# Stick-breaking attention regrouped into tiles of 4 query blocks by 512 keys, with the weights split into high and low parts for F32R products

## The chip, the cores and the metric

One core of one Trainium2 chip runs one launch of the kernel. The metric is the device time of that launch in microseconds (us). Everything is float32 in and out. F32R below is a reduced form of float32 that TensorE multiplies faster; where full precision is needed, the kernel keeps a number as a pair of F32R values, a high part and a low part (the remainder).

## The reference, cut to what matters

One layer of a hybrid encoder: 2048 tokens, width 1024. A projection feeds stick-breaking attention (8 heads of 64) and an mLSTM (4 heads of 128); both are gated, projected, normed and added, and a layer embedding is added last. The part that the change rewrites is the attention:

```python
for blk in range(s // SB_BLOCK):                      # 16 blocks of 128 queries
    q0 = blk * SB_BLOCK; k_end = q0 + SB_BLOCK
    z = jnp.einsum('bhqd,bhkd->bhqk', q[:, :, q0:k_end], k[:, :, :k_end]) * scale
    strict = s_pos < t_pos                            # a key strictly before its query
    log_beta = jax.nn.log_sigmoid(z)
    log_keep = jnp.where(strict, log_beta - z, 0.0)
    after = lax.cumsum(log_keep, axis=3, reverse=True) - log_keep
    a = jnp.where(strict, jnp.exp(log_beta + after), 0.0)
    outs.append(jnp.einsum('bhqk,bhkd->bhqd', a, v[:, :, :k_end]))
```

The cumulative sum runs over all keys of a query from the last to the first. A row that is cut into pieces of keys is therefore a chain: a piece begins with what the piece to its right ended with.

## The kernel before

The kernel is a row of stages, each a block in which five engines (TensorE = PE, VectorE = DVE, ScalarE = ACT, GpSimd = POOL, SyncE = SP for DMAs) run their own programs and meet at semaphores. `input_projection` multiplies the normed input by nine groups of 512 weight columns, as three F32R products each, and stores the results to DRAM. Groups 0 and 1 are queries and keys: ACT writes the high part (`evacuate_hi`), DVE the low part (`evacuate_lo`), and SP stores both (`store_qk`) from two staging buffers each. Group 2 is the values: `evacuate_copy` lets ACT and DVE copy alternate tiles, and SP stores them as rows of 2 KB into `proj_n`. A short block `prepare_mlstm` follows, then `stick_breaking_attention`, then `mlstm_and_output_projection`, then `layer_embedding`.

The attention works in units. A unit is one head, one block of 128 queries and up to 512 keys; a query block with more keys is cut into nearly equal pieces, taken from the right. There are 80 units for a pair of heads and 320 in all. A loop over the four pairs holds the code of 80 units (`pipeline`, with a part ahead of and behind the loop). At step n each engine works on units at fixed lags behind n:

- PE `score(n)`: two F32R products of queries with keys, 128 x 512, into one of four PSUM tiles `y`.
- ACT at lag 1: exp, then ln(1 + x), into `buf`.
- POOL at lag 2, for the first (rightmost) unit of a row alone: it adds `lowest` to the 128x128 diagonal block (line 708).
- DVE at lag 2: `softplus` (line 813), then `start`, which is one column: the negated last key (line 833) for a first unit, or what the unit to the right left, less the own last key (line 835).
- DVE at lag 3: `scan` (line 822), the running sum over the keys of the unit.
- POOL at lag 4, for first units: `lowest` is added once more (line 701).
- PE at lag 5: `turn` transposes every 128x128 block (line 734). ACT at lag 6: exp of the turned block into `aT` (line 786). PE at lag 7: `times_v` (line 761), for each block of keys a plain float32 product of `aT` (stationary) with the values of two heads, 128 columns. DVE at lag 8: a 128x64 copy of the finished output (line 849).

Each engine's queue is strictly in this written order. On DVE the order within a step is scan(n-3), softplus(n-2), start(n-2), and, where a row has ended, the copy. `score(u)` waits for `start(u-3)`, so for the scan of u-4, to free its tile `y`.

Of the kernel before, what the change touches and what calls it, by code (L numbers as in the profile page):

```python
# [43 lines left out]
def input_projection(nc, x, pre_norm_w, w_in, conv_w, conv_b, sb_norm_w, ml_norm_w, qk_hi, qk_lo, ml_t, proj_n,  # L44
# [8 lines left out]
    with ExitStack() as ctx:  # L53
# [140 lines left out]
        def _(sp):  # L194
# [12 lines left out]

            def store_first(q, j):
                store_qk(q - 1, j, slice(j * P, (j + 1) * P), bass.ds((q - 1) * GROUP, GROUP))
# [26 lines left out]
            with sp.Fori(0, TG) as m:  # L236
                for t in range(TG):
                    store_qk(m + TG, t, bass.ds((m + TG) * P, P), slice(t * GROUP, (t + 1) * GROUP))

# [9 lines left out]
            store(evacuated, 2, proj_n, 0, BANKS, 0)  # L249
# [3 lines left out]
            store(evacuated, 6, proj_n, 0, BANKS, 2 * GROUP)  # L253
            store(evacuated, 7, proj_n, 0, BANKS, 3 * GROUP)
            store(staged, 3, proj_n, 0, BANKS, 4 * GROUP)
# [4 lines left out]
            for t in range(BANKS):  # L260
                sp.wait_ge(stored[t], 16 * ((GROUPS - 2) * TG + 2))
            for i in range(2):
                sp.wait_ge(stored_hi[i], 16 * (4 * TG + 1))
                sp.wait_ge(stored_lo[i], 16 * (4 * TG + 1))

        @block.scalar
        def _(act):
# [38 lines left out]
            def evacuate_copy(g):  # L306
                def tile(m, t):
                    if t % 2 == 1:
                        act.wait_ge(out_ready, 4 * m + (16 * g + t + 2))
                        act.wait_ge(stored[t], 16 * m + (16 * ((g - 2) * TG + 1)))  # L310
                        nc.scalar.copy(stage[t], po[t][:]).then_inc(evacuated[t], 1)
                return tile

            def evacuate_gate(g, func):
                def tile(m, t):
                    act.wait_ge(out_ready, 4 * m + (16 * g + t + 2))
                    act.wait_ge(stored[t], 16 * m + (16 * ((g - 2) * TG + 1)))
                    nc.scalar.activation(stage[t], po[t][:], func).then_inc(evacuated[t], 1)
                return tile

            def evacuate_conv(g):
                def silu(m, t):
                    act.wait_ge(tap_done, TG * CONV_K * m + CONV_K * (TG * TG * (g - 4) + t + 3))
                    act.wait_ge(stored[t], 16 * m + (16 * ((g - 2) * TG + 1)))
# [32 lines left out]
            for g, evacuate in ((1, evacuate_hi(1, 1.0)),  # L357
                                (2, evacuate_copy(2)), (3, evacuate_gate(3, ACT.Silu)),
# [7 lines left out]
            for t in (1, 3):  # L366
                act.wait_ge(out_ready, 16 * GROUPS + (t + 2))
                act.wait_ge(stored[t], 16 * ((GROUPS - 2) * TG + 1))
# [3 lines left out]
        def _(dve):  # L372
# [37 lines left out]
            def evacuate_copy(g):  # L410
                def tile(m, t):
                    if t % 2 == 0:
                        dve.wait_ge(out_ready, 4 * m + (16 * g + t + 2))
                        dve.wait_ge(stored[t], 16 * m + (16 * ((g - 2) * TG + 1)))
# [56 lines left out]
            for g, evacuate in ((1, evacuate_lo(1, 1.0)),  # L471
                                (2, evacuate_copy(2)), (3, weigh_gate(3, gate_w[0])),
# [9 lines left out]
                if g == 4:  # L482
                    dve.wait_ge(conv_w_loaded, 16 * (CONV_K + 1))
                    for i in range(2):
                        dve.wait_ge(stored_hi[i], 16 * (4 * TG + 1))
                        dve.wait_ge(stored_lo[i], 16 * (4 * TG + 1))
                whole_group(dve.Fori, evacuate, (lambda ks: split(g + 1, ks)) if g < GROUPS - 1 else nothing)
            for t in (0, 2):
                dve.wait_ge(out_ready, 16 * GROUPS + (t + 2))
                dve.wait_ge(stored[t], 16 * ((GROUPS - 2) * TG + 1))  # L490
# [81 lines left out]
def stick_breaking_attention(nc, qk_hi, qk_lo, proj_n, y_sb, before, other_loads):  # L572

# [4 lines left out]
    with ExitStack() as ctx:  # L586
# [10 lines left out]
        BUFS, YS = 8, 4  # L597

        units = []
        for head in range(2):  # L600
            for i in range(TOK):

                parts = i // 4 + 1
                bounds = [(i + 1) * c // parts * P for c in range(parts + 1)]
                for c in reversed(range(parts)):
                    units.append((head, i, bounds[c], bounds[c + 1] - bounds[c], c == parts - 1, c == 0))
        UNITS = len(units)
        assert UNITS % BUFS == 0 and UNITS % YS == 0
        BEYOND_START = 4
        assert units[BEYOND_START][1] == 4  # L610
        firsts = [u for u in range(UNITS) if units[u][4]]

        E_LAG, SP_LAG, S_LAG, M_LAG, T_LAG, X_LAG, V_LAG, O_LAG = 1, 2, 3, 4, 5, 6, 7, 8

        def rank(u):

            return len(firsts) * (u // UNITS) + sum(f <= u % UNITS for f in firsts)

        def pipeline(fori, step):

            for n in range(O_LAG):
                step(0, n)
            with fori(0, PAIRS - 1) as it:
                for n in range(O_LAG, UNITS + O_LAG):
                    step(it, n)
            for n in range(O_LAG, UNITS + O_LAG):
                step(PAIRS - 1, n)

        def has(it, u):

            return u >= 0 and not (isinstance(it, int) and it == PAIRS - 1 and u >= UNITS)

# [3 lines left out]
        v = sb("b_v", [P, TOK, SB_WIDTH])  # L636
        buf = [sb(f"b_buf{s}", [P, GROUP]) for s in range(BUFS)]
        aT = [sb(f"b_aT{s}", [P, GROUP]) for s in range(2)]
        ident = sb("b_ident", [P, P])
        lowest = sb("b_lowest", [P, P])  # L640
# [3 lines left out]
        qk_loaded = [sem(f"qk_loaded{s}") for s in range(2)]  # L644
        start_loaded = sem("b_start_loaded")
        v_start_loaded = sem("b_v_start_loaded")
        v_loaded = sem("b_v_loaded")
# [3 lines left out]
        ln_masked = sem("ln_masked")  # L651
        sp_done = sem("sp_done")
        scan_done = sem("scan_done")
        log_done = sem("log_done")
        log_masked = sem("log_masked")
        turned_done = sem("turned_done")
        aT_done = sem("aT_done")
        av_done = sem("av_done")
        o_read = sem("o_read")
        def load_head(sp, s, head, cols, loaded):  # L660
            q, k = bass.ds(head * SB_DIM, SB_DIM), bass.ds(head * SB_DIM + SB_WIDTH, SB_DIM)
# [6 lines left out]
        def load_v(sp, tiles, loaded):  # L668
            rows = proj_n[tiles.start * P:tiles.stop * P, 0:SB_WIDTH]
            sp.dma_start(v[:, tiles, :], rows.rearrange("(j p) n -> p j n", p=P)).then_inc(loaded, 16)  # L670

        def prefetch(sp):

            load_head(sp, 0, 0, slice(0, GROUP), start_loaded)
            load_v(sp, slice(0, 4), v_start_loaded)
# [4 lines left out]
        o = [psum(f"b_o{s}", [P, P]) for s in range(2)]  # L680
# [3 lines left out]
        def _(pool):  # L684
            nc.gpsimd.memset(ident[:], 0.0).then_inc(zeroed, 1)
            nc.gpsimd.memset(lowest[:], 0.0).then_inc(zeroed, 1)
            pool.wait_ge(zeroed, 2)
# [3 lines left out]
            nc.gpsimd.affine_select(out=lowest[:], in_=lowest[:], compare_op=ALU.is_gt, fill=-BIG, base=0,  # L691
                                    pattern=[[-1, P]], channel_multiplier=1).then_inc(consts_ready, 1)
            pool.wait_ge(consts_ready, 2)

            def step(it, n):
                u = n - M_LAG
                if has(it, u) and units[u % UNITS][4]:
                    keys = units[u % UNITS][3]
                    own = buf[u % BUFS][:, keys - P:keys]
                    pool.wait_ge(log_done, it * UNITS + (u + 1 + YS))  # L700
                    nc.gpsimd.tensor_tensor(own, own, lowest[:], ALU.add).then_inc(log_masked, 1)  # L701
                n -= E_LAG
                if has(it, n) and units[n % UNITS][4]:

                    keys = units[n % UNITS][3]
                    own = buf[n % BUFS][:, keys - P:keys]
                    pool.wait_ge(ln_done, it * UNITS + (n + 1))
                    nc.gpsimd.tensor_tensor(own, own, lowest[:], ALU.add).then_inc(ln_masked, 1)  # L708

            pipeline(pool.Fori, step)  # L710

        @block.sync
        def _(sp):
            load_head(sp, 0, 0, slice(GROUP, SEQ), qk_loaded[0])
            load_v(sp, slice(4, TOK), v_loaded)
            load_head(sp, 1, 1, slice(0, SEQ), qk_loaded[1])
            other_loads(sp)
            with sp.Fori(1, PAIRS) as it:
                for s in range(2):

                    sp.wait_ge(y_done, (it - 1) * UNITS + UNITS // 2 * (s + 1))
                    load_head(sp, s, 2 * it + s, slice(0, SEQ), qk_loaded[s])

        @block.tensor
        def _(pe):
            def turn(it, u):
                keys, first = units[u % UNITS][3:5]
                if first:
                    pe.wait_ge(log_masked, it * len(firsts) + rank(u))
                else:  # L730
                    pe.wait_ge(log_done, it * UNITS + (u + 1 + YS))
                pe.wait_ge(aT_done, it * UNITS + (u + 1))
                for j in range(keys // P):
                    mm = pe.transpose(turned[u % 2][:, j * P:(j + 1) * P], buf[u % BUFS][:, j * P:(j + 1) * P],  # L734
                                      ident[:])
                mm.then_inc(turned_done, 1)

            def score(it, u):
                head, i, key0, keys, first, last = units[u % UNITS]
                very_first = isinstance(it, int) and it == 0  # L740
                if very_first and u == 0:
                    pe.wait_ge(start_loaded, 96)
                if u % UNITS in (0, UNITS // 2) and not (very_first and u == 0) or very_first and u == BEYOND_START:
                    pe.wait_ge(qk_loaded[head], 96 * it + (96 * (u // UNITS) + 96))
                pe.wait_ge(log_done, it * UNITS + (u + 1))
# [5 lines left out]
            def times_v(it, u):  # L751
                head, i, key0, keys, first, last = units[u % UNITS]
                if isinstance(it, int) and it == 0 and u == 0:
                    pe.wait_ge(v_start_loaded, 16)
                if u == BEYOND_START:
# [1061 lines left out]
```

## Time and profile before

| | |
|---|---|
| median of 3 runs | 2082.02 us (2081.91 to 2086.26) |
| span of the profiled execution | 2080.1 us |
| input projection | 0 to 856 us |
| preparation of the mLSTM | 856 to 872 us |
| attention | 872 to 1502 us |
| mLSTM and output projection | 1502 to 1826 us |
| layer embedding | 1826 to 2080 us |
| PE, DVE, ACT, POOL busy over the span | 93%, 53%, 42%, 12% |

The span runs from the first to the last instruction. The busy share of an engine is a mean over stages with different limits, so it is read stage by stage. PE's busy time counts a matmul from its start to its modelled end, and matmuls overlap; the spacing of the weight loads (PEld) tells more of its pace.

### The profile page before, as it was taken

What the parts mean: (1) busy time and instruction counts of PE and PEld (TensorE: products, weight loads), DVE (VectorE), ACT (ScalarE), POOL (GpSimd) and SP (SyncE); (2) the same over time, 40 slices, a digit from 0 to 9 for tenths busy, and PEclk for the clock granted to TensorE, in tenths of its full rate; (3) what the DMA queues carried; (4) which work ended last, traced back from release to release, by engine and by line L of the source; (5) the groups of instructions that cost most, each with busy time, mean ns of one, the idle gap of its engine ahead of it and who ended that gap; (6) DMA issues with size and microseconds to landing.
All of it is one profiled execution on the core that took longest, in us unless ns stands there. A gap on an engine that the chain in (4) does not pass through costs nothing. (4 is left out here: it accounts for less than half of the span.)

```text
span 2080.1 us, 31157 instructions
## 1 busy us (share of the span) xinstructions
PE 1937.3 (93%) x10348; PEld 1612.5 (78%) x10348; DVE 1105.3 (53%) x2017; ACT 869.2 (42%) x1729; POOL 258.2 (12%) x442
## 2 busy tenths in 40 slices
PE   6999999999999999599989989999889999979998
PEld 5888888887878888277877777777768888858887
DVE  4521111355511011289989989999866555443333
ACT  4311111222201121188878878888644444331111
POOL 2100000000000000112112112112013344300000
PEclk9999999999999999799999999999969999989999
DMA  4653221212122111352202202100064444332221
GB/s 163 181 163 100 98 77 59 86 46 86 51 90 87 50 46 50 92 140 62 49 15 62 46 19 62 43 20 1 25 194 127 152 151 151 132 134 91 72 87 41
DMA packets 89296, 176.91 MB, mean 85 GB/s; under 512 B 12388, under 2 KB 39204, under 8 KB 86484
## 3 DMA queue, kind: packets, MB, share of 16 engines
q1 hardware_dynamic: 84344, 156.48, 24.7%
q0 software_dynamic: 4832, 18.91, 2.6%
q8 instruction: 66, 1.08, 0.2%
q14 instruction: 54, 0.44, 0.1%
HBM read 112.35 MB, written 63.01 MB: 84 GB/s over the span
## 5 line engine op out<-in xcount | busy, mean ns | idle before, releaser
L822 DVE TENSOR_TENSOR_SCAN b_buf<-b_y,b_buf 128x511 f32<-128x511 f32 (+2 forms) x320 | 357.4, 1117 | 16.8 <-issue 9.1
L761 PE MATMUL b_o<-b_v,b_aT 128*128 (+1 forms) x2176 | 299.2, 277 | 5.3 <-DVE y_sb L849 5.2
L761 PEld LDWEIGHTS b_o<-b_v,b_aT 128*128 128x128 f32 x2176 | 270.3, 193 | 10.2 <-issue 5.2
L548 PE MATMUL a_po<-w_lo,uT_hi 128*128 128x512 f32 x640 | 249.8, 390 | 2.4 <-DVE w_lo L398 2.4
L548 PE MATMUL a_po<-w_hi,uT_lo 128*128 128x512 f32 x640 | 249.7, 390 | 0.0
L548 PE MATMUL a_po<-w_hi,uT_hi 128*128 128x512 f32 x640 | 249.6, 390 | 0.0
L748 PE MATMUL b_y<-kst,qst_lo 128*128 128x512 f32 (+2 forms) x320 | 149.4, 467 | 52.0 <-DVE b_buf L835 27.4
L786 ACT ACTIVATE b_aT<-b_turned 128x512 f32<-128x512 f32 (+2 forms) x320 | 169.7, 530 | 63.0 <-PE b_o L761 47.4
L790 ACT ACTIVATE b_buf<-b_y 128x512 f32<-128x512 f32 (+2 forms) x320 | 169.9, 531 | 59.6 <-PE b_y L749 55.2
L813 DVE SCALAR_TENSOR_TENSOR b_buf<-b_buf,b_y 128x512 f32<-128x512 f32 (+2 forms) x320 | 186.2, 582 | 11.2 <-POOL b_buf L708 11.2
L734 PE MATMUL b_turned<-b_ident,b_buf 128*128 128x128 f32 x1088 | 176.9, 278 | 11.5 <-issue 8.9
L793 ACT ACTIVATE b_buf<-b_buf 128x512 f32<-128x512 f32 (+2 forms) x320 | 181.2, 566 | 10.1
L734 PEld LDWEIGHTS b_turned<-b_ident,b_buf 128*128 128x128 f32 x1088 | 131.9, 142 | 51.7 <-POOL b_buf L701 21.2
L548 PE MATMUL a_po<-uT_hi,w_lo 128*128 128x512 f32 x384 | 150.3, 391 | 2.4 <-DVE w_lo L398 2.4
L548 PE MATMUL a_po<-uT_lo,w_hi 128*128 128x512 f32 x384 | 149.9, 390 | 0.0
L548 PE MATMUL a_po<-uT_hi,w_hi 128*128 128x512 f32 x384 | 149.9, 390 | 0.0
L548 PEld LDWEIGHTS a_po<-w_lo,uT_hi 128*128 128x128 f32 x640 | 120.4, 188 | 27.8 <-DVE w_lo L398 2.8
L548 PEld LDWEIGHTS a_po<-w_hi,uT_hi 128*128 128x128 f32 x640 | 120.5, 188 | 25.3
L548 PEld LDWEIGHTS a_po<-w_hi,uT_lo 128*128 128x128 f32 x640 | 120.6, 188 | 24.9
L1684 PE MATMUL d_product<-d_w_hi,d_hT_lo 128*128 128x512 f32 x320 | 127.0, 397 | 3.8 <-DVE d_w_lo L874 3.6
L748 PEld LDWEIGHTS b_y<-kst,qst_lo 128*128 128x128 f32 x320 | 61.5, 192 | 88.1 <-DVE b_buf L835 53.1
L1684 PE MATMUL d_product<-d_w_hi,d_hT_hi 128*128 128x512 f32 x320 | 125.3, 391 | 0.0
(195 smaller groups left out, 3088.4 us busy)
## 6 DMA issues: line engine op xcount, KB each, us to landing
proj_n<-x_in SPq DMA_DIRECT2D x80, 256.0 KB
w_raw<-in_w_in POOLq DMA_DIRECT2D x8, 2048.0 KB, 9.5
x_in<-in_x SPq DMA_DIRECT2D x16, 512.0 KB, 4.3
qk_hi<-stage_hi SPq DMA_DIRECT2D x32, 256.0 KB, 2.5
qk_lo<-stage_lo SPq DMA_DIRECT2D x32, 256.0 KB, 3.1
ml_t<-x_in SPq DMA_DIRECT2D x32, 256.0 KB
ring<-ml_t SPq DMA_DIRECT2D x16, 512.0 KB, 4.7
ring<-proj_n SPq DMA_DIRECT2D x16, 512.0 KB, 4.1
```

What stands on the lines that cost most here:

```text
L548: mm = pe.matmul(po[t][:], lhsT, rhs, start=(k == 0 and n == 0), stop=(k == KT - 1 and n == 2))
L734: mm = pe.transpose(turned[u % 2][:, j * P:(j + 1) * P], buf[u % BUFS][:, j * P:(j + 1) * P], ident[:])
L748: pe.matmul(out, qst_lo[head][:, q], k, start=True, stop=False)
L761: mm = pe.matmul(o[i % 2][:], aT[u % 2][:, j * P:(j + 1) * P], v[:, key0 // P + j, bass.ds((it + u // UNITS) * P, P)], start=(first and j ...
L786: nc.scalar.activation(aT[x % 2][:, 0:keys], turned[x % 2][:, 0:keys], ACT.Exp).then_inc(aT_done, 1)
L790: nc.scalar.activation(b, y[e % YS][:, 0:units[e % UNITS][3]], ACT.Exp).then_inc(e_done, 1)
L793: nc.scalar.activation(b, b, ACT.Ln, bias=1.0).then_inc(ln_done, 1)
L813: nc.vector.scalar_tensor_tensor(out=b, in0=b, scalar=LN_MAX, in1=y[u % YS][:, 0:keys], op0=ALU.min, op1=ALU.max).then_inc(sp_done, 1)
L822: nc.vector.tensor_tensor_scan(down, y[u % YS][:, 1:keys][:, ::-1], down, b[:, keys - 1:keys], ALU.add, ALU.subtract)\
L1684: mm = pe.matmul(product[b][:], a[s][:, k, :], w[:, k, half], start=(k == ks[0] and i == 0), stop=(k == ks[-1] and i == 2))
```

## The change

In `stick_breaking_attention` the order of the units changes: for each head and each group g of 4 query blocks, the chunks c of 512 keys are taken from the right, and within a chunk the 4 query blocks r. A first unit (c = g) has (r + 1) x 128 keys, all others have 512. It is still 40 units a head and 320 in all, with the same keys in all. 24 of 40 are chained to the unit 4 places back. Besides units there are jobs, 40 a head too: a job is one block of 128 keys by the 4 query blocks of its chunk, so up to 512 columns wide (512, 384, 256 and 128 in the diagonal chunk).

- `pipeline` is written out over all 320 units with no loop, and lags grow: 15 steps instead of 8.
- The causal mask: POOL's two additions per first unit go. PE adds `future` (BIG above the diagonal) to the tile `y` with one BF16 product per first unit, after ACT's exp has read it (`hide_future`); POOL sets one column with a memset (`mask_end`).
- DVE's one-column instruction: none for a first unit; for a chained one a `tensor_tensor` of two SBUF columns (`seed`). What the earlier unit left is put into `carry` by ACT (`carry_over`, one column, 192 times).
- After the exp of a job, POOL splits the 128 x up to 512 weights: a copy rounded to F32R (`hi`), then a subtraction (`lo`). PE multiplies with the pair of values as the stationary operand, two F32R products of up to 512 columns per job. The result `o` is 128 (high and low halves of 64) x 512 queries.
- When a group of query blocks ends, ACT copies `o` (`copy_o`), PE turns it with 4 transposes (`turn_o`), DVE adds the halves (`add_o`). It happens 32 times and takes the place of 128 copies.
- In `input_projection`, group 2 is evacuated as a pair like groups 0 and 1 and stored to `v_pair` in pieces of 256 bytes; the attention loads 1 MB of it per head, in pieces of 512 bytes, instead of 4 MB once.

The core of the diff (waits on `stored`, columns of `proj_n` and declarations of semaphores are left out):

```diff
+            def store_v(m, t):
+                i, n = t % 2, m + 2 * TG
+                rows = bass.ds((m * BANKS + t) * P, P)
+                sp.wait_ge(staged_hi[i], 2 * n + (t // 2 + 1))
+                sp.dma_start(v_pair[:, rows, 0, :].rearrange("h p d -> p h d"),
+                             stage_hi[i][:, 0:GROUP].bitcast(F32).rearrange("p (h d) -> p h d", h=SB_HEADS))\
+                    .then_inc(stored_hi[i], 16)
...
-                                (2, evacuate_copy(2)), (3, evacuate_gate(3, ACT.Silu)),
+                                (2, evacuate_hi(2, 1.0)), (3, evacuate_gate(3, ACT.Silu)),
...
-        BUFS, YS = 8, 4
+        BUFS, YS, PARTS = 12, 4, 3
...
+            for g in range(TG):
+                for c in reversed(range(g + 1)):
+                    for r in range(4):
+                        keys = (r + 1) * P if c == g else GROUP
+                        units.append((head, 4 * g + r, c * GROUP, keys, c == g, c == 0))
+                        r0 = r if c == g else 0
+                        jobs.append((head, 4 * c + r, r0 * P, c == g and r == 0, c == 0 and r == 3))
...
-        E_LAG, SP_LAG, S_LAG, M_LAG, T_LAG, X_LAG, V_LAG, O_LAG = 1, 2, 3, 4, 5, 6, 7, 8
+        E_LAG, F_LAG, SP_LAG, S_LAG, C_LAG, T_LAG, X_LAG, H_LAG, V_LAG, R_LAG, W_LAG, O_LAG = 1, 2, 2, 3, 4, 8, 9, 10, 12, 13, 14, 15
...
+            for n in range(PAIRS * UNITS + O_LAG):
+                step(n)
...
-                    nc.gpsimd.tensor_tensor(own, own, lowest[:], ALU.add).then_inc(log_masked, 1)
+            def split(m):
+                cols = slice(jobs[m % UNITS][2], GROUP)
+                raw, hi, lo = aT[m % 2][:, cols], a_hi[m % PARTS], a_lo[m % PARTS]
+                pool.wait_ge(aT_done, m + 1)
+                until(pool, av_done, (m - PARTS + 1))
+                nc.gpsimd.tensor_copy(hi[:, cols], raw).then_inc(hi_done, 1)
+                pool.wait_ge(hi_done, m + 1)
+                nc.gpsimd.tensor_tensor(lo[:, cols], raw, hi[:, cols].bitcast(F32), ALU.subtract).then_inc(lo_done, 1)
...
+            def hide_future(u):
+                    pe.wait_ge(e_done, u + 1)
+                    pe.matmul(y[u % YS][:, keys - P:keys], ident_b[:], future[:], start=False, stop=True,
+                              skip_group_check=True).then_inc(future_hidden, 1)
...
+                pe.matmul(o[:, col:], pair, a_lo[m % PARTS][:, col:], start=first, stop=False)
+                pe.matmul(o[:, col:], pair, a_hi[m % PARTS][:, col:], start=False, stop=last).then_inc(av_done, 1)
...
+            def step(n):
+                if has(n - C_LAG):
+                    carry_over(n - C_LAG)
+                if has(n - R_LAG):
+                    copy_o(n - R_LAG)
+                if has(n - X_LAG):
+                    weights(n - X_LAG)
+                if has(n - E_LAG):
+                    log_one_plus_exp(n - E_LAG)
...
-                    nc.vector.tensor_scalar_mul(last_key, last_key, -1.0).then_inc(log_done, 1)
...
+                if not units[u % UNITS][4]:
+                    last_key, before = buf[u % BUFS][:, GROUP - 1:GROUP], (u - 4) % 8
+                    dve.wait_ge(sp_done, u + 1)
+                    dve.wait_ge(carried, passed(carrying, u - 3))
+                    nc.vector.tensor_tensor(last_key, carry[:, before:before + 1], last_key, ALU.subtract)\
+                        .then_inc(seed_done, 1)
```

## Rows read from the trace of the kernel before

**Rows 1.** Stages: each engine's busy us (instructions), then TensorE clock, DMA share, GB/s.

```profile
872.00:1502.00 630.00, 562.61 (x3903) 481.60 (x3904) 587.41 (x1087) 496.42 (x961) 115.27 (x258) 0.97 0.21 48
```

**Rows 2.** Groups by shape in the attention: busy us, mean ns of one, idle before.

```profile
L822 DVE TENSOR_TENSOR_SCAN b_buf<-b_y,b_buf 128x511 f32<-128x511 f32 x160 | 204.4, 1278 | 4.8 <-DVE b_buf L833 0.9
L835 DVE SCALAR_TENSOR_TENSOR b_buf<-b_y,b_buf 128x1 f32<-128x1 f32 x192 | 42.0, 219 | 6.8
L786 ACT ACTIVATE b_aT<-b_turned 128x512 f32<-128x512 f32 x160 | 95.5, 597 | 40.7 <-PE b_o L761 36.2
```

**Rows 3.** DVE in order of time in the middle of the attention: start, us, instruction.

```profile
1246.11 0.22 DVE L835 SCALAR_TENSOR_TENSOR b_buf<-b_y,b_buf 128x1 f32<-128x1 f32 x1
1246.36 1.01 DVE L822 TENSOR_TENSOR_SCAN b_buf<-b_y,b_buf 128x383 f32<-128x383 f32 x1
1247.29 0.66 DVE L813 SCALAR_TENSOR_TENSOR b_buf<-b_buf,b_y 128x512 f32<-128x512 f32 x1
1247.99 0.15 DVE L833 TENSOR_SCALAR b_buf<-b_buf 128x1 f32<-128x1 f32 x1
1248.18 1.28 DVE L822 TENSOR_TENSOR_SCAN b_buf<-b_y,b_buf 128x511 f32<-128x511 f32 x1
```

**Rows 4.** Waits of 900 to 1500 us: us in total, times, longest.

```profile
DVE b_buf L822 <- issue: 9.1, 2, 4.8
```

**Rows 5.** Short instructions of DVE and one reduction, from the groups by shape.

```profile
L1510 DVE TENSOR_TENSOR c_den<-c_den,c_cols 128x4 f32<-128x4 f32 x16 | 2.6, 165 | 1.6
L849 DVE COPY y_sb<-b_o 128x64 f32 x96 | 20.8, 217 | 1.1 <-PE b_o L761 0.7
L1468 DVE TENSOR_REDUCE c_ss<-c_squares 128x8 f32<-128x512 f32 x16 | 10.8, 676 | 0.0
```

**Rows 6.** Groups by shape of POOL.

```profile
L701 POOL TENSOR_TENSOR b_buf<-b_buf,b_lowest 128x128 f32<-128x128 f32 x128 | 58.5, 457 | 347.1 <-DVE b_buf L835 331.1 <-DVE b_buf L833 15.1
L1418 POOL TENSOR_TENSOR c_rstd<-c_ss,c_minus_half 128x12 f32<-128x12 f32 x16 | 36.5, 2282 | 1.2
L1420 POOL TENSOR_TENSOR c_y<-c_y,ring 128x512 f32<-128x512 f32 x16 | 21.3, 1332 | 21.2 <-DVE c_y L1476 21.2
L989 POOL TENSOR_SCALAR_AFFINE_SELECT c_sel<-c_sel 4x512 f32<-4x512 f32 x1 | 0.6, 629 | 0.0
L977 POOL MEMSET c_state<- 128x528 f32 x1 | 0.5, 527 | 0.0
L688 POOL TENSOR_SCALAR_AFFINE_SELECT b_ident<-b_ident 128x128 f32<-128x128 f32 x1 | 0.3, 292 | 0.1
```

**Rows 7.** Line 1481, where POOL's line 1420 starts alongside: ns min/median/max.

```profile
L1481 DVE SCALAR_TENSOR_TENSOR c_y<-c_num,c_rstd,ring x64: 336/342/1387, 1529.9 to 1795.7; 128x128 f32<-128x128 f32 x64
```

**Rows 8.** PE's weight loads and a one-column instruction of ACT.

```profile
1245.38 0.97 PEld L761 LDWEIGHTS b_o<-b_v,b_aT 128*128 128x128 f32 x8
L1381 ACT ACTIVATION_READ_ACCUMULATOR c_junk<-c_out 128x1 f32 x32 | 6.2, 194 | 0.0
```

**Rows 9.** Windows as in rows 1: projection, attention's start, and two more.

```profile
180.00:262.00 82.00, 82.00 (x364) 67.89 (x363) 13.02 (x20) 11.54 (x20) 0.88 (x1) 1.00 0.31 102
879.00:889.00 10.00, 3.17 (x11) 2.56 (x12) 2.25 (x5) 2.43 (x7) 0.93 (x3) 0.50 1.02 288
1242.00:1248.00 6.00, 5.94 (x47) 5.31 (x46) 5.79 (x13) 5.18 (x11) 0.92 (x2) 1.00 0.01 3
1522.00:1527.00 5.00, 3.69 (x15) 3.06 (x16) 3.99 (x9) 2.36 (x7) 1.27 (x2) 0.50 0.52 162
```

**Rows 10.** The attention's end in order of time.

```profile
1497.51 1.28 DVE L822 TENSOR_TENSOR_SCAN b_buf<-b_y,b_buf 128x511 f32<-128x511 f32 x1
1502.35 0.23 DVE L849 COPY y_sb<-b_o 128x64 f32<-128x64 f32 x1 [3.44 <-PE b_o L761]
```

**Rows 11.** DMA issues: count, KB each, median us to landing.

```profile
qk_lo<-stage_lo SPq DMA_DIRECT2D x32, 256.0 KB, 3.1
ring<-ml_t SPq DMA_DIRECT2D x16, 512.0 KB, 4.7
```

More of the change, by code:

```diff
@@ L596, in stick_breaking_attention @@
         PAIRS = SB_HEADS // 2
-        BUFS, YS = 8, 4
-        units = []
+        BUFS, YS, PARTS = 12, 4, 3
+        units, jobs, groups = [], [], []
         for head in range(2):
[L601 to L607, printed above, removed]
@@ new lines, in stick_breaking_attention @@
+        UNITS, GROUPS_OF_PAIR = len(units), len(groups)
+        assert UNITS % BUFS % 4 == 0 and UNITS % YS == 0 and UNITS % 2 == 0
+        firsts = [u for u in range(UNITS) if units[u][4]]
+        chained = [u for u in range(UNITS) if not units[u][4]]
+        carrying = [u for u in range(UNITS) if not units[u][5]]
+        ends = [m for m in range(UNITS) if jobs[m][4]]
+        MASK = BIG
+        E_LAG, F_LAG, SP_LAG, S_LAG, C_LAG, T_LAG, X_LAG, H_LAG, V_LAG, R_LAG, W_LAG, O_LAG = 1, 2, 2, 3, 4, 8, 9, 10, 12, 13, 14, 15
@@ L710, in _, with mask_end @@
-            pipeline(pool.Fori, step)
+            def mask_end(u):
+                keys, first = units[u % UNITS][3:5]
+                if first:
+                    until(pool, turned_done, last_job_of(u - BUFS))
+                    nc.gpsimd.memset(buf[u % BUFS][:, keys - 1:keys], -MASK).then_inc(ends_masked, 1)
+            def split(m):
[6 more added lines that the diff above has]
+                nc.gpsimd.tensor_tensor(lo[:, cols], raw, hi[:, cols].bitcast(F32), ALU.subtract).then_inc(lo_done, 1)
@@ L712, in _ @@
+            def step(n):
+                if has(n):
+                    mask_end(n)
+                if has(n - H_LAG):
+                    split(n - H_LAG)
+            pipeline(step)
         @block.sync
@@ L760, in times_v @@
-                for j in range(keys // P):
-                    mm = pe.matmul(o[i % 2][:], aT[u % 2][:, j * P:(j + 1) * P],
-                                   v[:, key0 // P + j, bass.ds((it + u // UNITS) * P, P)],
-                                   start=(first and j == 0), stop=(last and j == keys // P - 1))
-                mm.then_inc(av_done, 1)
-            def step(it, n):
-                if has(it, n - T_LAG):
-                    turn(it, n - T_LAG)
-                if has(it, n - V_LAG):
-                    times_v(it, n - V_LAG)
-                if has(it, n):
-                    score(it, n)
@@ new lines, in carry_over, with weights @@
+            def carry_over(u):
+                if not units[u % UNITS][5]:
+                    act.wait_ge(log_done, u + 1)
+                    nc.scalar.activation(carry[:, u % 8:u % 8 + 1], y[u % YS][:, 0:1], ACT.Identity,
+                                         bias=buf[u % BUFS][:, 0:1]).then_inc(carried, 1)
+            def weights(m):
+                cols = slice(jobs[m % UNITS][2], GROUP)
+                act.wait_ge(turned_done, m + 1)
+                until(act, lo_done, (m - 1))
+                nc.scalar.activation(aT[m % 2][:, cols], turned[m % 2][:, cols], ACT.Exp).then_inc(aT_done, 1)
@@ new lines, in log_one_plus_exp @@
+            def log_one_plus_exp(u):
+                keys, first = units[u % UNITS][3:5]
+                cols = slice(0, keys - 1 if first else keys)
+                b = buf[u % BUFS][:, cols]
+                act.wait_ge(y_done, u + 1)
+                until(act, turned_done, last_job_of(u - BUFS))
+                nc.scalar.activation(b, y[u % YS][:, cols], ACT.Exp).then_inc(e_done, 1)
+                act.wait_ge(e_done, u + 1)
+                nc.scalar.activation(b, b, ACT.Ln, bias=1.0).then_inc(ln_done, 1)
@@ L816, in scan @@
-            def scan(it, u):
-                keys = units[u % UNITS][3]
                 b = buf[u % BUFS]
                 down = b[:, 0:keys - 1][:, ::-1]
-                dve.wait_ge(log_done, it * UNITS + (u + YS))
-                nc.vector.tensor_tensor_scan(down, y[u % YS][:, 1:keys][:, ::-1], down,
-                                             b[:, keys - 1:keys], ALU.add, ALU.subtract)\
-                    .then_inc(log_done if not has(it, u + 1) else scan_done, 1)
-            def start(it, u):
+                if first:
+                    dve.wait_ge(sp_done, u + 1)
+                    dve.wait_ge(ends_masked, passed(firsts, u) + 1)
+                else:
+                    dve.wait_ge(seed_done, passed(chained, u) + 1)
@@ new lines, in add_o @@
+            def add_o(m):
+                head, block_of_keys, col, first, last = jobs[m % UNITS]
+                if last:
+                    k, g = passed(ends, m), groups[passed(ends, m) % len(groups)][1]
+                    dve.wait_ge(o_turned, k + 3)
+                    nc.vector.tensor_reduce(y_sb[:, 4 * g:4 * g + 4, m // UNITS * P + head * SB_DIM:m // UNITS * P + (head + 1) * SB_DIM],
+                                            o_rows[:].rearrange("p r b d -> p r d b"), AX.X, ALU.add).then_inc(o_read, 1)
@@ L855, in split_weights, with step @@
+            def step(n):
+                if has(n - S_LAG):
+                    scan(n - S_LAG)
+                if has(n - SP_LAG):
+                    softplus(n - SP_LAG)
+                    seed(n - SP_LAG)
+                if has(n - O_LAG):
+                    add_o(n - O_LAG)
+            dve.sem_inc(o_turned, 2)
+            dve.sem_inc(o_read, 1)
+            pipeline(step)
 def split_weights(nc, tiles, raw, hi, lo, loaded, hi_done, lo_done):
```

281 lines of the change are left out of this document (140 added, 141 removed).

## The prediction

> **What bounds the kernel now.** I read the windows by stage first. The attention takes 630 us, and DVE is busy for 587 of them while ACT is busy for 496 and POOL for 115 [rows 1]. PE shows 563 us of busy time, but that counts overlapping matmuls, so I went on to the order of time on DVE. There the instructions stand without a gap: scan, softplus, one column, scan, each start within 0.03 us of what it depends on [rows 3]. The chain of waits by the page stays in the last stage, so for the attention the bound is read from this order: **DVE sets the pace**. A unit of 512 keys costs it 1.20 us of scan up to the next start (1.28 us long, overlapping by 0.08), 0.70 us of softplus and 0.19 or 0.25 us for the one column, about 2.13 us [rows 2, 3]. PE's weight loads come in runs with room between them.
>
> What else is in the 630 us: two pauses of DVE of together 9.1 us that nothing in the profile releases, at the loop's returns [rows 4]; about 8 us idle at the start, where DVE works 2.25 of 10 us while the DMA engines are full, because unit 4 waits for its keys and queries [rows 9]; and 3.8 us from the last scan's end (1498.8) to the last copy's end (1502.6) [rows 10]. The projection is PE-bound: 364 products in 82 us, 0.225 us apart, with DVE busy 13 us and ACT 11.5 [rows 9].
>
> **The change, part by part.** All terms are in us on the profiled span of 2080.1; the runs' median of 2082.0 lies 1.9 above it.
>
> *DVE, scans and softplus.* The number of units and of keys is the same, and both instructions cost a fixed part plus a part per key, so the regrouping alone moves nothing: 0.
>
> *DVE, one column.* For 128 first units line 833 goes, with 0.19 from its start to the scan's [rows 3]: 128 x 0.19 = **-24**. For 192 chained units a scalar_tensor_tensor of 0.219 [rows 2] becomes a tensor_tensor; the nearest row is 0.165 for 4 columns [rows 5]: -0.05 x 192 = **-10** (0 at worst).
>
> *DVE, output.* 128 copies of 0.217 go [rows 5]. They mostly fall into the wait between the one column and the scan; I value them at 0.08, estimated between nothing and their whole length, so -10. 32 reductions of 512 elements at 0.676 [rows 5], less an overlap of 0.05, give +20. Together **+10** (-8 to +20).
>
> *No loop.* The two pauses go: **-9**. Inside the loop's body the code of 80 units already ran in a straight line without such a pause, so I expect none in its place.
>
> *Start.* The values loaded ahead of the first heads' other keys shrink from 1 MB to 256 KB. At 288 GB/s [rows 9] that is 2.7 us less in front of unit 4: **-2** (-3 to 0).
>
> *PE.* Products with plain float32 weights: 8 loads in 0.97 us, 0.11 apart [rows 8], so 0.89 us for a full job; in their place stand two F32R products of 512 columns at 0.225 [rows 9], 0.45 us. The masks (128 short BF16 products) and 32 x 4 transposes add little. A full job costs PE about 0.45 + 0.45 + 0.45 = 1.35 us, where DVE takes 2.1. PE was not the bound, so this saving, 0.44 x 272 = 120 us of PE (272 is 1088 blocks over 4), is worth nothing by itself: 0.
>
> *ACT.* 192 one-column instructions at the 0.19 of its nearest row [rows 8] and 32 copies of 0.6 (as the 128x512 exp [rows 2]) add 36 + 19 = 55 to its 496: 551 of about 640. It stays below DVE, but now both `score` (through `carried`) and the next unit wait for it. I charge **+5** for waits that meet (0 to 55).
>
> *POOL.* This is the step that decides. POOL's additions go (2 x 128 x 0.457 = 117 [rows 6], hidden behind DVE), and every job brings a copy and a subtraction. The subtraction is priced: 1.332 for 128x512, 0.457 for 128x128 [rows 6]. The copy has no row. Nearest from below is a memset, 0.527 for 528 columns; nearest in kind, one input and one output, is the affine_select, 0.629 for 512 columns and 0.292 for 128; from above, the two-input 1.332 [rows 6]. I take 0.63. Between two dependent instructions POOL idles 1.2 us over 16, 0.08 each [rows 6]. A full job: 0.63 + 0.08 + 1.33 = 2.04. By straight lines through the same rows, jobs of 384, 256 and 128 columns cost 1.64, 1.23 and 0.82. In all 224 x 2.04 + 32 x 3.69 = 575, and 128 memsets of at most 0.1 make 588. DVE comes to about 607 - 24 = 583 (630 less 9, 8, 4 and 2 at the edges is 607; -24 is the sum of its terms). **Two engines are then equally full**, and coupled through ACT and PE. In the diagonal tiles POOL needs 2.04 + 1.64 + 1.23 + 0.82 = 5.7 for four jobs where DVE needs 5.2 for four units; of 32 x 0.5 = 16 I count **+12** (0 to 16).
>
> The Trainium skill's page GPSIMD Engine Reference, section 4.1 Engine selection, advises against elementwise work there: about 2 times VectorE's time with two inputs, roughly line rate with one. The rows agree for two inputs: POOL's 1.332 is twice DVE's 0.66 for a softplus of 512 [rows 3, 6]. By that rule the copy lies near 0.63 and not near 1.33; no row here shows it.
>
> *DVE against POOL.* Line 1481 on DVE reads two SBUF tensors. Of its 64 instructions the median is 0.342 us, the longest 1.387 and the sum 34.7 us in place of 22; at its place POOL's line 1420 (1.33 us) has just started [rows 6, 7]. So a DVE instruction with two SBUF inputs stands still until POOL's is done, while the scan and softplus, which read one input from PSUM, do not grow beside line 701. `seed` is such an instruction with two SBUF inputs, 192 times, and POOL will be almost always busy. How long it waits depends on the phase. From the end of scan(u): ACT's carry_over, which waits for it, and the exp of a job end about 0.83 later; POOL copies (0.63), pauses (0.08), subtracts (1.33) and is done at 2.87. DVE's softplus ends and the next seed is ready at 0.62 of its period T. So the wait is w = 2.87 - T - 0.62 with T = 2.12 + w, which gives w = 0.07. I take 0.1 for handing over: 192 x 0.1 = **+19** (0 to 96, the mean wait at a random phase being (0.63^2 + 1.33^2)/(2 x 2.12) = 0.5).
>
> The Trainium skill's page SBUF — State Buffer, section Who interferes with whom, says this outright: the second input comes through the read interface shared with GpSimd, and the later instruction blocks fully. The trace agrees, with 1.387 against 0.342. Taken with no phase lock, that is the rival of the random phase below.
>
> *Drain.* Behind the last scan stand now some 6 jobs of POOL, 12, and then two products, a copy, 4 transposes and a reduction, about 3: 15 in place of 3.8, **+12** (4 jobs: +7; 8 jobs: +16).
>
> *Projection.* DVE and ACT evacuate the values as they do groups 0 and 1, under a full PE [rows 9]. A store in 1024 pieces of 256 bytes has no row; 256 KB in 2 KB pieces land in 3.1, and 1024 pieces of 512 bytes in 4.7 [rows 11]. Two stores per tile of 24 x 0.225 = 5.4 us with two buffers each have 10.8 to land: 0. If pieces were the limit so that a tile took 7.2, it would be +29.
>
> Sum: -24 - 10 + 10 - 9 - 2 + 5 + 12 + 19 + 12 = **+13**: a span of 2093, a median of **2095 us**, +0.6%.
>
> **The rivals.**
> - *Faster: the phases fit (0.23).* DVE stays the bound, seeds find POOL between instructions, POOL keeps up in the diagonal tiles. Then -24 - 10 + 10 - 9 - 2 + 8 = -27, a median of 2055; with half of each loss, 2075. It decides as soon as lock, diagonal tiles and ACT cost together under 23 us. For it: POOL's jobs are queued two deep and DVE is synchronised with them. Against: POOL would be busy 588 of 600.
> - *POOL is the bound (0.21).* The copy, which rounds, costs more than 0.63. Each 0.1 more is 27 us once POOL is fuller than DVE. At 0.98, halfway to the subtraction's price, POOL needs 588 + 95 = 683, plus 12 until its first job and 3 at the end: attention 698, total 2150. At 1.33 it is 2245.
> - *Seeds wait at random phase (0.07).* 96 in place of 19: 2172.
> - *PE's clock (0.06).* The granted clock is 1.00 of 2.4 GHz while PE is busy 5.94 of 6 us, and 0.50 (1.2 GHz) where it was busy 3.69 of 5 with gaps [rows 9]. With 1.35 us of work in 2.15 PE could lose its clock; a full job then costs 2.7, and 272 x 2.7 = 734 makes about 2190. Against it: the gaps are below a microsecond, and a slower PE fills them itself.
> - *The stores bound group 2 (0.03).* +29 on mine: 2124.
>
> **How the numbers follow.** My forecast has 0.40; its own range is 2080 to 2115. Runs of this kernel differ by about 0.2% (4 us) with no change. Below 2078 lie most of the faster rival and none else: 0.21. Between 2078 and 2086 lie the lower edge of mine and the upper of the rival: 0.12. The rest, 0.67, is slower. For 8 in 10 I leave out the lowest of the faster case (0.07) and the dearer half of the POOL case with the tails (0.13): 2060 to 2150.
>
> **What would show it.** Right: DVE without gaps but for seeds, whose mean is 0.25 to 0.35 and whose shortest is near 0.17; a POOL copy of 128x512 near 0.63 and POOL busy near 590 in an attention of about 643; no 4.8 us pauses; 10 to 17 us between the last scan and the last reduction; group 2 as fast as group 1. Wrong in price: DVE waiting on ACT, ACT on POOL, POOL without gaps. Wrong in phase: seeds near 0.6. Wrong in clock: a granted clock below 1.00 in the middle of the attention. Wrong in the stores: PE waiting in group 2.

## The result and the profile after

The changed kernel takes 2134.5 us (2134.0 to 2137.4) against 2082.1 of the kernel before: a ratio of 1.0249, interval 1.0235 to 1.0264. The forecast was 2095. The direction was right, and the time lies in the range of 8 in 10 (2060 to 2150), but outside the forecast's own 2080 to 2115; the size, +52, was four times the +13 that the sum gave. The profiled execution spans 2135.7 us, 55.6 more than before. It was the longest of the four executions (2137.4), so some 3 of the 55.6 are the spread between executions.

First the windows by stage of the changed kernel (columns as in [rows 1]): the projection, in which group 2 is now a pair, two stretches of it (the second holds all 32 stores of group 2), the attention's start and its middle.

```profile
0.00:856.00 856.00, 830.54 (x3680) 677.30 (x3680) 239.37 (x371) 187.59 (x316) 24.47 (x53) 1.00 0.30 92
180.00:262.00 82.00, 82.00 (x364) 67.89 (x363) 15.79 (x24) 13.98 (x24) 0.88 (x1) 1.00 0.46 123
215.00:310.00 95.00, 95.00 (x420) 78.64 (x419) 19.54 (x30) 18.01 (x31) 1.77 (x2) 1.00 0.52 124
879.00:889.00 10.00, 3.96 (x15) 2.85 (x16) 3.55 (x6) 3.00 (x8) 0.00 (x0) 0.50 1.08 239
880.00:1540.00 660.00, 505.37 (x2578) 359.84 (x2579) 623.11 (x857) 519.05 (x1171) 514.60 (x749) 0.90 0.21 49
```

The projection still ends at 856 us, and PE has no gap in either stretch. The stores of the values, in pieces of 256 bytes, land as fast as those of queries and keys [rows 11]:

```profile
v_pair<-stage_hi SPq DMA_DIRECT2D x16, 256.0 KB, 2.6
v_pair<-stage_lo SPq DMA_DIRECT2D x16, 256.0 KB, 2.8
```

DVE is busy for 623 of 660 us of the attention: it is still what the attention waits for. POOL is busy for 515. PE's clock, 0.98 before between 880 and 1500 us, is down to 0.90.

Then the groups by shape of the changed kernel's DVE and POOL, against [rows 2, 5, 6]:

```profile
L882 DVE TENSOR_TENSOR_SCAN b_buf<-b_y,b_buf 128x511 f32<-128x511 f32 x224 | 286.6, 1279 | 7.4
L901 DVE TENSOR_TENSOR b_buf<-b_carry,b_buf 128x1 f32<-128x1 f32 x192 | 89.0, 463 | 6.6
L909 DVE TENSOR_REDUCE y_sb<-b_o_rows 128x256 f32<-128x512 f32 x32 | 21.8, 682 | 14.3 <-PE b_o_rows L807 14.3
L730 POOL TENSOR_TENSOR b_a_lo<-b_aT,b_a_hi 128x512 fp32r<-128x512 f32 x224 | 287.0, 1281 | 17.9
L728 POOL CAST b_a_hi<-b_aT 128x512 fp32r<-128x512 f32 x224 | 136.8, 611 | 61.8 <-PE b_o L799 37.2 <-ACT b_aT L838 22.9
L721 POOL MEMSET b_buf<- 128x1 f32 x128 | 12.2, 98 | 0.0
```

Both prices of POOL were near: the copy 0.611 (forecast 0.63), the subtraction 1.281 (1.33). The scan is as long as before. The seed is not as forecast: one column takes 0.463 us on average. The same instruction by its line gives the spread (ns min/median/max):

```profile
L901 DVE TENSOR_TENSOR b_buf<-b_carry,b_buf x192: 158/202/1291, 893.3 to 1538.4; 128x1 f32<-128x1 f32 x192
```

And here is the order of time of DVE, then of POOL, around one of them (start, us, instruction):

```profile
1204.30 0.66 DVE L892 SCALAR_TENSOR_TENSOR b_buf<-b_buf,b_y 128x512 f32<-128x512 f32 x1
1204.99 0.92 DVE L901 TENSOR_TENSOR b_buf<-b_carry,b_buf 128x1 f32<-128x1 f32 x1
1205.95 1.28 DVE L882 TENSOR_TENSOR_SCAN b_buf<-b_y,b_buf 128x511 f32<-128x511 f32 x1
```

```profile
1203.92 0.61 POOL L728 CAST b_a_hi<-b_aT 128x512 fp32r<-128x512 f32 x1
1204.61 1.28 POOL L730 TENSOR_TENSOR b_a_lo<-b_aT,b_a_hi 128x512 fp32r<-128x512 f32 x1
1205.84 0.09 POOL L721 MEMSET b_buf<- 128x1 f32 x1
```

POOL's subtraction ends at 1205.89, the seed at 1205.91, and the softplus ahead of it, with one SBUF input, ran its usual 0.66 beside POOL's work. Setting the start of each of the 192 seeds in the trace against POOL's copies and subtractions: 70 start beside neither and take 0.160 on average; 48 start within a copy and take 0.357; 74 start within a subtraction and take 0.820. In the median those of the two latter kinds end 0.015 to 0.016 us behind POOL's instruction. In all 192 x (0.463 - 0.160) = **58 us**.

### The profile page after: what moved, and what is told of

Same layout as the page of the kernel before. It is cut to its first block and busy times, and to the rows that moved or that the text cites. A ratio compares the mean times of both kernels' runs of the same rounds, so it can differ in the third digit from the quotient of the medians.

```text
span 2135.7 us, 28530 instructions
## 1 busy us (share of the span) xinstructions
PE 1894.9 (89%) x9068; PEld 1501.3 (70%) x9068; DVE 1150.2 (54%) x1801; ACT 904.2 (42%) x1961; POOL 669.3 (31%) x956
## 5 line engine op out<-in xcount | busy, mean ns | idle before, releaser
L730 POOL TENSOR_TENSOR b_a_lo<-b_aT,b_a_hi 128x512 fp32r<-128x512 f32 (+1 forms) x320 | 357.1, 1116 | 25.6
L728 POOL CAST b_a_hi<-b_aT 128x512 fp32r<-128x512 f32 (+1 forms) x320 | 174.9, 547 | 127.4 <-PE b_o L799 96.7
L777 PEld LDWEIGHTS b_y<-kst,qst_lo 128*128 128x128 f32 x320 | 67.2, 210 | 193.9 <-DVE b_buf L882 148.2
L892 DVE SCALAR_TENSOR_TENSOR b_buf<-b_buf,b_y 128x512 f32<-128x512 f32 (+2 forms) x320 | 186.9, 584 | 25.3 <-PE b_y L785 15.7
L763 PE MATMUL b_turned<-b_ident,b_buf 128*128 128x128 f32 x1088 | 192.1, 296 | 4.3 <-DVE b_buf L882 2.1
L838 ACT ACTIVATE b_aT<-b_turned 128x512 f32<-128x512 f32 (+1 forms) x320 | 169.0, 528 | 44.6 <-POOL b_a_lo L730 40.7
L191 POOL DMA_DIRECT2D w_raw<-in_w_in x8 | 7.1, 888 | 558.9 <-DVE w_lo L413 558.5
L798 PE MATMUL b_o<-b_a_lo,b_v 128*128 128x512 f32 (+1 forms) x320 | 154.5, 483 | 21.7 <-ACT b_o_sb L855 11.9
L763 PEld LDWEIGHTS b_turned<-b_ident,b_buf 128*128 128x128 f32 x1088 | 137.0, 154 | 39.1 <-issue 24.6
L563 PEld LDWEIGHTS a_po<-w_hi,uT_lo 128*128 128x128 f32 x640 | 120.5, 188 | 25.2
```

Source lines behind the costliest of these rows:

```text
L563: mm = pe.matmul(po[t][:], lhsT, rhs, start=(k == 0 and n == 0), stop=(k == KT - 1 and n == 2))
L728: nc.gpsimd.tensor_copy(hi[:, cols], raw).then_inc(hi_done, 1)
L730: nc.gpsimd.tensor_tensor(lo[:, cols], raw, hi[:, cols].bitcast(F32), ALU.subtract).then_inc(lo_done, 1)
L763: mm = pe.transpose(turned[m % 2][:, r * P:(r + 1) * P], buf[(tile + r) % BUFS][:, key:key + P], ident[:])
L777: pe.matmul(out, qst_lo[head][:, q], k, start=True, stop=False)
L798: pe.matmul(o[:, col:], pair, a_lo[m % PARTS][:, col:], start=first, stop=False)
```

## The experiments

Each is compared with runs of the kernel before on the same chip.

**The seed with one SBUF tensor.** The subtraction becomes a multiplication by -1 and the addition of a pointer scalar.

```diff
-                    nc.vector.tensor_tensor(last_key, carry[:, before:before + 1], last_key, ALU.subtract)\
+                    nc.vector.tensor_scalar(last_key, last_key, -1.0, carry[:, before:before + 1], ALU.mult, ALU.add)\
```

> The changed kernel with one edit: the seed is a tensor_scalar on one SBUF column, times -1 plus the carried column as a pointer scalar, in place of a tensor_tensor of two SBUF columns. Theory A (the shared read path: seeds stand behind POOL's instruction and DVE sets the pace): the 192 seeds fall from a mean of 0.463 us to 0.15 to 0.22, 47 to 57 us less on DVE, and the median falls from 2134.5 to 2075 to 2095, the upper end if part of it comes back as waits for POOL or ACT. Theory B (POOL, ACT and PE together set the pace, and the seeds only stand where DVE would wait anyway): seeds get short, the gaps ahead of softplus grow by as much, and the median stays at 2120 or above. Theory C (a pointer scalar takes the shared path too): seeds stay at 0.40 or more and the time does not change.

Measured: 2081.6 us, ratio 0.9992 (0.9981 to 1.0003). This one edit takes 53 us off and brings the kernel back to the time of before. The instruction's line in this run:

```profile
L901 DVE TENSOR_SCALAR b_buf<-b_buf,b_carry x192: 212/214/217, 893.7 to 1483.2; 128x1 f32<-128x1 f32 x192
```

None of the 192 is longer than 0.217, though POOL does the same work at their side. That is 48 us less on DVE (192 x (0.463 - 0.214)), and the rest is fewer waits: the idle time before softplus is 19.2 us in place of 25.3. Theory A holds; B and C fall. The window of the attention in this run:

```profile
880.00:1485.00 605.00, 464.00 (x2578) 327.58 (x2579) 573.90 (x857) 513.80 (x1170) 513.98 (x749) 0.98 0.23 54
```

PE's clock came back too, from 0.90 to 0.98, with the same products in less time. So this run alone does not tell the seeds from the clock. But a slow PE can reach DVE only as a wait, and DVE's waits for PE and ACT before softplus changed by 6 of the 53 us.

**More work for PE.** The first product of `score` is issued twice.

```diff
-                pe.matmul(out, qst_lo[head][:, q], k, start=True, stop=False)
+                pe.matmul(out, qst_lo[head][:, q], k, start=True, stop=True)
+                pe.matmul(out, qst_lo[head][:, q], k, start=True, stop=False)
```

> The changed kernel with more work for PE: the first of the two products in score is issued twice (the repeat starts the sum anew, so the output is the same), 320 x 0.22 = 70 us of PE more. Theory A (shared path on DVE): granted clock of the attention rises from 0.89, seeds stay at a mean of 0.40 to 0.50 us, and the time stays within 2125 to 2140. Theory D (PE's lost clock makes the loss, since 151 us of the attention run at 1.2 GHz and POOL waits 97 us for PE): the clock rises to 0.97 or more, POOL's wait for PE's products falls below 50 us, and the time falls by 15 us or more.

Measured: 2133.0 us, ratio 1.0227 (1.0207 to 1.0247). The window of the attention's middle in this run shows the clock at 0.94 in place of 0.90, and DVE as full as before:

```profile
880.00:1540.00 660.00, 537.14 (x2893) 402.62 (x2893) 618.83 (x857) 517.33 (x1171) 515.65 (x750) 0.94 0.21 49
```

The seeds' mean is 0.446 and POOL's wait for PE's products 97.3 us, about as with the lower clock (0.463 and 96.7). With two levels, 2.4 and 1.2 GHz, a mean of 0.90 over 660 us is some 130 us at 1.2 GHz, and 0.94 some 80. The clock rose less than theory D asked for, and the added products cost PE time themselves, so this run bounds the matter rather than closing it: with 50 us less at 1.2 GHz the time fell by 1.5 us, no more than single executions differ.

**Earlier products.** The products with the values and all behind them one step earlier.

```diff
-        ... V_LAG, R_LAG, W_LAG, O_LAG = ... 12, 13, 14, 15
+        ... V_LAG, R_LAG, W_LAG, O_LAG = ... 11, 12, 13, 14
```

> The changed kernel with the products with the values, the copy, the turn and the reduction one step earlier (lags 11, 12, 13, 14 in place of 12, 13, 14, 15). POOL's wait for PE's products (97 us in the profile) should fall to a third of that. Theory A: that wait is not on the path, so the time moves by less than 8 us either way, and only the phase between seeds and POOL changes, with the seeds' mean between 0.35 and 0.55 us. Theory B (POOL's chain sets the pace): the time falls by 15 us or more.

Measured: 2124.8 us, ratio 1.0181 (1.0154 to 1.0208): 10 us less than the changed kernel, a little more than theory A allowed and less than B asked. POOL's longest waits between 880 and 1550 us (us in total, times, longest), first in the changed kernel:

```profile
POOL b_a_hi L728 <- PE b_o L799: 96.7, 69, 3.5
POOL b_a_hi L728 <- ACT b_aT L838: 28.9, 28, 17.4
```

Then with the earlier products, and below it the seeds of that run:

```profile
POOL b_a_hi L728 <- ACT b_aT L838: 110.4, 112, 17.8
```

```profile
L901 DVE TENSOR_TENSOR b_buf<-b_carry,b_buf 128x1 f32<-128x1 f32 x192 | 75.0, 391 | 6.6
```

POOL is now released by ACT's exp, as the forecast had assumed, and the seeds lose 192 x (0.391 - 0.160) = 44 us in place of 58. The softplus gives part of these 14 us back: its waits for PE and ACT in the same stretch grow from 21.8 to 25.2 us. Together that is the gain of 10.

**Pointer seed with earlier products.**

> The seed with one SBUF tensor and a pointer scalar, and the products with the values one step earlier, together. Theory A (the shared path only; the earlier products gained 10 us because they moved POOL's instructions against the seeds, whose loss fell from 57 to 44 us): with no seed left to stand behind POOL, the earlier products gain nothing more, 2078 to 2083 as with the pointer seed alone. Theory B (the earlier products shorten a chain through POOL that is on the path by itself): 2068 to 2074.

Measured: 2082.5 us, ratio 1.0004 (0.9994 to 1.0014). With no seed that can stand behind POOL the earlier products bring nothing: their 10 us were the lock's.

**A spare instruction with two SBUF inputs,** behind each pointer seed:

```diff
+                    nc.vector.tensor_tensor(spare[:], carry[:, before:before + 1], ident[:, 0:1], ALU.subtract)
```

> The changed kernel with the pointer seed (2081.6), and right behind each of the 192 seeds one spare tensor_tensor on DVE of two SBUF columns into a spare column. Its own length is 0.16 us, 0.1 to 0.16 to the next start. Theory A (an instruction with two SBUF inputs stands behind POOL's): its mean is 0.35 to 0.50 us and the time rises by 50 to 95 us, to 2132 to 2177. If there is no such standing: a mean of 0.16 us, and a rise of 19 to 31 us, to 2100 to 2113.

Measured: 2137.8 us, ratio 1.0249 (1.0229 to 1.0269), 56 us more than with the pointer seed alone. Its groups by shape show the pointer seeds and the spare instructions:

```profile
L902 DVE TENSOR_SCALAR b_buf<-b_buf,b_carry 128x1 f32<-128x1 f32 x192 | 41.2, 215 | 6.8
L904 DVE TENSOR_TENSOR b_spare<-b_carry,b_ident 128x1 f32<-128x1 f32 x192 | 85.2, 444 | 0.0
```

The cost was taken away and given back by an instruction that nothing depends on, while the pointer form just ahead of it stays at 0.215.

**The end.** Pointer seed, and the copies and subtractions of the last 7 jobs on DVE.

```diff
+        ON_DVE = PAIRS * UNITS - 7
-                if has(n - H_LAG):
+                if has(n - H_LAG) and n - H_LAG < ON_DVE:
                     split(n - H_LAG)
...
```

DVE's program gets the same copy and subtraction for these 7 jobs (left out here).

> The pointer seed, and the splits of the last 7 jobs on DVE, which is idle for 15 us there, in place of POOL. A 128x512 copy and subtraction on DVE take about 0.4 and 0.69 us against POOL's 0.61 and 1.28, 0.8 us a job: the drain of 15 us should fall to 9 to 11 and the median to 2074 to 2078. If the drain is set by the exps and products between the splits, it stays at 2080 to 2082.

Measured: 2078.5 us, ratio 0.9980 (0.9970 to 0.9989). DVE took 0.423 for the copy and 0.692 for the subtraction. The gain was 3 us, just short of what was expected. From the last scan's end to the last reduction's it now takes 11.6 us, against 15.5 with the pointer seed alone; 9 to 11 was expected. With the earlier products as well:

> Pointer seed, earlier products and the last 7 splits on DVE. Theory A: as the kernel with the tail alone, 2073 to 2078. Theory B: 2062 to 2070, which would beat the kernel before and its version without the loop (2069.7).

Measured: 2077.2 us, ratio 0.9971 (0.9959 to 0.9984), as theory A had it.

**One part alone: no loop, on the kernel before.**

```diff
-            with fori(0, PAIRS - 1) as it:
+            for it in range(PAIRS - 1):
```

> The kernel before with one part of the change alone: the loop over pairs of heads is written out in straight line. The two pauses of 4.8 us on DVE go and nothing comes in their place: 9 us less, a median of 2071 to 2075. If instructions have to be fetched in straight line as well, the time stays at 2080 to 2084.

Measured: 2069.7 us, ratio 0.9930 (0.9913 to 0.9946), 12.8 us less than the kernel before on the same chip: a little more than the two pauses of together 9.1, and more than was expected. No wait of DVE without a releaser is left.

**Fewer products, on the kernel before.** Every second block of keys is left out of the products with the values, so the attention's output is incomplete.

```diff
-                for j in range(keys // P):
+                kept = range(0, keys // P, 2)
+                for j in kept:
```

> The kernel before, which leaves out every second block of keys in the products of weights and values (the output of the attention is then incomplete): some 43% of those products go, about 100 us of PE. The prediction held PE's saving to be worth nothing in the attention, since DVE sets the pace: 2078 to 2083. If PE's time counts, it falls by 10 us or more; if PE loses its clock and waits meet, it rises by 5 or more.

Measured: 2081.3 us, ratio 0.9991 (0.9981 to 1.0001). The window from 900 to 1500 us of this run:

```profile
900.00:1500.00 600.00, 467.48 (x2881) 367.55 (x2879) 571.32 (x1053) 471.72 (x928) 108.83 (x242) 0.99 0.17 37
```

PE's time in the products is worth nothing while DVE is full: busy for 571 of 600 us.

**Two parts alone: no loop and the mask by TensorE, on the kernel before.** The core of the edit:

```diff
-                    nc.gpsimd.tensor_tensor(own, own, lowest[:], ALU.add).then_inc(log_masked, 1)
-                    nc.gpsimd.tensor_tensor(own, own, lowest[:], ALU.add).then_inc(ln_masked, 1)
+                    nc.gpsimd.memset(buf[n % BUFS][:, keys - 1:keys], -BIG).then_inc(ends_masked, 1)
...
+                    pe.matmul(y[u % YS][:, keys - P:keys], ident_b[:], future[:], start=False, stop=True,
+                              skip_group_check=True).then_inc(future_hidden, 1)
...
-                    nc.vector.tensor_scalar_mul(last_key, last_key, -1.0).then_inc(log_done, 1)
```

> The kernel before without its loop (2069.7), plus one more part of the change alone: the mask by one BF16 product of TensorE and one memset per first unit, in place of two additions on POOL and the negated column on DVE. Units, products, copies and chaining as before. If the prediction's term for the column holds on a DVE that sets the pace (128 x 0.19 = 24 us): 2043 to 2050. If first units now wait for the mask product behind PE's queue: 2055 to 2070.

Measured: **2044.4 us**, ratio 0.9814 (0.9795 to 0.9832), 25 us less than with the loop written out alone (24 by the two ratios; the runs are from different chips). DVE in order of time:

```profile
1241.10 0.22 DVE L847 SCALAR_TENSOR_TENSOR b_buf<-b_y,b_buf 128x1 f32<-128x1 f32 x1
1241.36 1.28 DVE L836 TENSOR_TENSOR_SCAN b_buf<-b_y,b_buf 128x511 f32<-128x511 f32 x1
1242.55 0.26 DVE L823 SCALAR_TENSOR_TENSOR b_buf<-b_buf,b_y 128x127 f32<-128x127 f32 x1
1242.85 0.48 DVE L836 TENSOR_TENSOR_SCAN b_buf<-b_y,b_buf 128x127 f32<-128x127 f32 x1
1243.25 0.40 DVE L823 SCALAR_TENSOR_TENSOR b_buf<-b_buf,b_y 128x255 f32<-128x255 f32 x1
```

A first unit now goes from softplus to scan with nothing between. This is the fastest version of the study. It has the two parts with the largest gains of the sum, the pauses and the negated column. It does without the split on POOL, which saves time of PE alone, and PE had time to spare.

## Why the prediction was wrong in size

The steps, each by what DVE's order of time and the groups show, on the profiled spans:

| step | forecast | measured |
|---|---|---|
| negated column gone | -24 | -24; alone -25 |
| seed shorter, without standing | -10 | -12 (192 x 0.160 + 6.6 idle, before 42.0 + 6.8) |
| seeds behind POOL | **+19** | **+58** |
| copies against reductions | +10 | about +8 |
| pauses of the loop | -9 | -9; alone -13 |
| start | -2 | about 0 |
| ACT's waits and diagonal tiles | +5 and +12 | +14 (idle before softplus 25.3, before 11.2) |
| drain | +12 | +11 (15.0 from 1539.84, before 3.8) |
| scans and softplus | 0 | about +3 (less overlap) |
| projection | 0 | 0 |
| behind the attention | 0 | +3 |
| sum | +13 | +52; the span grew by 55.6 |

The measured column is rounded and partly estimated from overlaps, so it adds up to the span's growth only within some 4 us.

**The step that failed** is "DVE against POOL": the mechanism was right, and the term was mis-sized at 0.1 us a seed where 0.30 was measured. That is 39 us, as much as the two sums (+13 and +52) lie apart. The other terms are off by 3 at most, and it is luck that their errors cancel. With the pointer seed, which cannot stand and takes 0.214 in place of 0.160, the rest of the sum is tested without the failed term: 2095 - 19 + 10 = 2086, and 2081.6 was measured. The working of the failed term assumed a fixed phase: carry_over and the exp of a job end 0.83 us behind a scan and release POOL, so that POOL's subtraction ends just as the seed is ready. The trace shows another releaser: for 69 of POOL's waits, 96.7 us, it is PE's product with the values three jobs back, and for 28, 28.9 us, the exp. With the releaser that I had assumed (the earlier products, 112 waits on the exp) a seed still lost 0.23 on average. So even then the phase does not hold: 63 of that run's seeds found neither of POOL's instructions running, 40 the copy and 89 the subtraction. The mean wait at a random phase, 0.5, overstated the loss of the changed kernel as much as the fixed one understated it; what each wait's phase comes from is not settled by these runs.

The Trainium skill's page SBUF — State Buffer, section Who interferes with whom, gives the mechanism as the prediction cited it: the second SBUF input of a VectorE instruction comes through the read interface shared with GpSimd. These runs agree: the seeds that met POOL's work end 0.015 us behind it in the median. The Trainium skill's page DVE: scalar operands, raw-bit mode, write accounting and state across instructions, section 1. Scalar operands, adds what the prediction did not use: a pointer scalar does not take up the second tensor stream. The 192 pointer seeds of at most 0.217 agree.

Point by point otherwise. DVE set the pace before and after. PE's saving was worth nothing, shown by leaving products out. POOL was not the bound: its jobs cost 570 us against the 588 of the forecast, 544 of them busy (357.0 + 175.0 + 12.2) and 25.7 idle between copy and subtraction. The clock was lost for part of the attention (0.90), which the prediction held for unlikely; by the runs above its share in the loss is small: at most 6 us through waits of DVE, and 3 us of seeds (0.446 against 0.463) in the run with more work for PE. The stores in 256-byte pieces stayed hidden: they landed in 2.6 and 2.8 us, at most 7.8 of the 10.8 that the forecast allowed, and PE is busy for all of the 95 us in which they were issued. The random-phase rival missed this one term by as much above (96 against 58) as my own value did below (19), and I had given it 0.07 by treating the phase as either fixed or random.

Open: the +3 us behind the attention. A 512 KB load from `proj_n` lands there in 4.8 us in place of 4.1. It takes 4.7 to 5.1 in the other versions of the changed kernel and 3.8 to 4.0 in those of the kernel before, so the difference is steady, but its cause was not tried by itself.

## What to carry to other kernels

Before work goes to GpSimd, go through VectorE's instructions beside it for those with two SBUF inputs. Each can cost up to a whole GpSimd instruction, however short it is itself (up to 1.291 us here for one column). Value it by how often GpSimd is busy rather than by a hoped-for phase: here 122 of 192 met GpSimd's work, and the mean loss was 0.30 us. One operand as a pointer scalar (0.217 at most) or from PSUM (the softplus, 0.654 to 0.680 in all 192 of 512 keys) took the cost away. Take from a large change the parts that shorten the engine that sets the pace, and try them alone: here two of them gave -38 us (2044.4 against 2082.1), and the change as a whole +52.

## What the runs showed of the hardware

- A one-column tensor_tensor of two SBUF inputs on DVE took 0.158 to 1.291 us, and as a tensor_scalar with a pointer scalar 0.212 to 0.217, beside the same work on GpSimd.
- GpSimd's rounding copy of 128x512 to F32R took 0.611 us, its subtraction 1.281. On VectorE the same two took 0.423 and 0.692.
- TensorE's granted clock, which has the two levels 2.4 and 1.2 GHz, fell to a mean of 0.90 with PE busy for 505 of 660 us in the changed kernel. It was 0.98 with PE busy for 464 of 605 us with the pointer seed, and 0.99 with 467 of 600 when products were left out of the kernel before.
- Stores of 256 KB in pieces of 256 bytes landed in 2.6 and 2.8 us in the median.
